# Cached keys turned in 32x32 blocks on VectorE and moved into place by on-chip transfers, instead of 128 TensorE turnings with copies

## The reference

```
ki_past = cache_idx_k[page_table]            # (8, 2048, 64) indexer keys
s     = einsum('bqhd,bsd->bqhs', qi, ki_all) * 64**-0.5
score = einsum('bqh,bqhs->bqs', wi * 8**-0.5, relu(s))
_, sel = top_k(score, 256)
ksel, vsel = cache_k / cache_v rows of sel   # (.., 64)
logits = einsum('bqhd,bqkd->bqhk', q, ksel) * 64**-0.5 ; softmax ; times vsel
```

## Time and profile before

| | |
|---|---|
| median of 3 runs | 1207.28 us |
| the profiled execution | 1206.73 us |
| its span on the core | 1204.9 us |
| mean granted TensorE clock | 0.995 |
| PE busy | 1144.1 us (95%) |
| DVE busy | 374.9 us (31%) |
| ACT busy | 223.7 us (19%) |
| POOL busy | 57.3 us (5%) |
| DMA | 451.92 MB, mean 375 GB/s |

### The profile page before, as it was taken

One profiled execution on the slowest core, in us unless ns is written; L12 is line 12 of the kernel. 1 busy time (PEld: TensorE's weight loads), 2 busy tenths in 40 slices (PEclk: granted clock), 3 DMA queues, 4 the chain that ended last, 5 costly groups with the idle time before them and its releaser, 6 DMA issues.

```text
span 1204.9 us, 15008 instructions
## 1 busy us (share of the span) xinstructions
PE 1144.1 (95%) x5865; PEld 508.8 (42%) x5865; DVE 374.9 (31%) x888; ACT 223.7 (19%) x449; POOL 57.3 (5%) x71
## 2 busy tenths in 40 slices
PE   7998999999999999999999999999989898999997
PEld 6776568773333333333333333333323333333332
DVE  2279942534231322222222223122212222222222
ACT  2236641442111111111111111111111111111102
POOL 2138100000000000000000000000000000000000
PEclk9999999999999999999999999999999999999999
DMA  9345447797999999999999999999999999999994
GB/s 371 106 146 211 168 145 290 297 412 280 404 429 428 426 427 429 426 427 427 428 428 427 427 428 429 426 426 428 428 426 430 427 426 428 427 427 428 429 426 205
DMA packets 44245, 451.92 MB, mean 375 GB/s; under 512 B 5516, under 2 KB 6440, under 8 KB 18055
## 3 DMA queue, kind: packets, MB, share of 16 engines
q1 hardware_dynamic: 41695, 436.94, 86.7%
q0 software_dynamic: 2480, 14.02, 3.1%
HBM read 448.56 MB, written 2.61 MB: 374 GB/s over the span
## 4 chain that ended last, share of the span: by engine, by line
PE 59%; DMA 25%; DVE 12%; ACT 3%; issue 1%; SPq 0%; DVEq 0%; ACTq 0%
DMA mem<-in_w_up_dram 25%; PE psum L1258 20%; PE psum L1295 15%; PE psum L724 4%; PE psum L1245 3%; PE psum L1033 2%; DVE mem L2239 2%; PE psum L1209 2%; PE psum L931 1%; DVE mem L2231 1%; DVE mem L2234 1%; PE psum L1236 1%; ACT mem L1706 1%; DVE mem L2236 1%; PE psum L1223 1%
## 5 line engine op out<-in xcount | busy, mean ns | idle before, releaser
L1258 PE MATMUL psum<-mem 128*64 128x512 f32 x2048 | 457.4, 596 | 13.7 <-DMA mem<-in_w_up_dram 13.2
L1258 PEld LDWEIGHTS psum<-mem 128*64 128x64 f32 x2048 | 142.6, 137 | 303.8 <-issue 274.7
L1295 PE MATMUL psum<-mem 128*64 128x512 f32 x1024 | 236.9, 600 | 0.0
L1295 PEld LDWEIGHTS psum<-mem 128*64 128x64 f32 x1024 | 66.5, 136 | 133.2 <-issue 112.6
L2231 DVE TENSOR_SCALAR mem<-psum 128x512 f32<-128x512 f32 x32 | 22.2, 693 | 275.1 <-PE psum L1258 275.1
L1706 ACT ACTIVATE mem<-mem 128x512 f32<-128x512 f32 x32 | 20.2, 631 | 467.2 <-DVE mem L2231 467.2
L2226 DVE TENSOR_TENSOR mem<-mem,psum 128x528 f32<-128x528 f32 x64 | 45.2, 706 | 130.1 <-PE psum L1245 130.1
L1432 ACT ACTIVATE mem<-psum 128x512 f32<-128x512 f32 (+6 forms) x125 | 61.0, 550 | 97.6 <-PE psum L724 40.9
L1245 PE MATMUL psum<-mem 128*128 128x264 f32 x256 | 65.5, 398 | 0.0
L2216 DVE TENSOR_SCALAR mem<-mem 128x64 f32<-128x64 f32 x99 | 25.0, 312 | 126.9 <-PE psum L1230 99.4
L1201 PE MATMUL psum<-mem 128*64 128x512 f32 x256 | 60.4, 592 | 1.0 <-DVE mem L2147 1.0
(11 more groups left out here) (355 smaller groups left out, 859.8 us busy)
## 6 DMA issues: line engine op xcount, KB each, us to landing
mem<-in_w_up_dram SPq DMA_DIRECT2D x128, 2048.0 KB, 32.5
mem<-in_w_down_dram SPq DMA_DIRECT2D x64, 2048.0 KB, 33.8
mem<-in_w_in_dram SPq DMA_DIRECT2D x8, 868.0 KB, 15.5
mem<-in_cache_mem_k_dram SPq DMA_DIRECT2D x1, 4096.0 KB, 19.9
mem<-in_cache_mem_v_dram SPq DMA_DIRECT2D x1, 4096.0 KB, 15.0
mem<-in_w_o_dram SPq DMA_DIRECT2D x1, 3072.0 KB, 10.9
mem<-in_w_mk_dram SPq DMA_DIRECT2D x2, 1024.0 KB, 6.8
mem<-in_w_mv_dram SPq DMA_DIRECT2D x1, 2048.0 KB, 10.5
```

The source lines that it names most:

```text
L1258: ins = pe.matmul(ps[64 * o:64 * o + 64, :], lhs, w[:, k % 2, g * 1024 + o * 512:g * 1024 + (o + 1) * 512], start=False, stop=(k == 7), sk ...
L1295: ins = pe.matmul(pso[64 * o:64 * o + 64, :], lhs, w[:, k % 4, o * 512:(o + 1) * 512], start=(k == 0), stop=(k == 7), skip_group_check=True)
```

## The change

Nothing is turned on TensorE any more: the jobs `kt`, the buffer `both`, GpSimd's copies and ScalarE's `keep_keys` are gone. `blocks` takes the place of `both`. VectorE's `turn_blocks(q)` makes two transposes per quarter (keys, index keys), each of 128 partitions x 2048 elements, in squares of 32 x 32. A square stays on its 32 partitions, so 16 transfers a quarter, issued by SP, put the squares in place in `KT`: 32 partitions x 4 KB each, from partitions 32g to partitions 32 b4. Columns of `KT` are now (group, position, page), and the views that read them follow. VectorE turns quarter 0 ahead of its first rotation, 1 after the second, 2 after the `QB` copies, 3 between the prompt's two selections. Each waits for the gathers of its quarter and for all transfers of the quarter before (`keys_moved`), since `blocks` has one buffer. SP waits for both transposes, and for quarters 2 and 3 also for `sl` q - 2, which read the same `KT`. GpSimd's gather q waits for the transposes of q - 1. `sample_logits(q)` waits for the transfers of quarter q. In TensorE's order `z` 2 comes ahead of `kin`, `z` 5 ahead of `kvn`, `sl` 0 and 1 ahead of `z` 7 and 8, and `sc` 0 behind the prompt logits.

```diff
@@ -158,15 +158,12 @@
 def psum_jobs():
     js = [("xT", k) for k in range(KD)]
     js += [("z", m) for m in Z_FIRST] + [("rs",)]
-    js += [("z", 1), ("sw", 13), ("sw", 9), ("kin",), ("wr",)] + [("kt", i) for i in range(4)]
-    js += [("z", 2), ("sw", 10), ("sw", 11)] + [("kt", i) for i in range(4, 8)]
-    js += [("z", 3), ("sw", 12), ("sw", 4), ("sw", 0), ("kvn",), ("z", 5), ("sw", 1), ("sw", 2), ("sw", 3)]
-    js += [("kt", i) for i in range(8, 12)] + [("is", 0, g, o) for g in range(2) for o in range(2)]
-    js += [("z", 6)] + [("kt", i) for i in range(12, 16)] + [("is", 1, g, o) for g in range(2) for o in range(2)]
-    js += [("z", 7), ("z", 8)]
-    js += [("sl", 0)] + [("kt", i) for i in range(16, 24)]
-    js += [("sl", 1), ("sc", 0)] + [("kt", i) for i in range(24, 32)]
-    js += [("sl", 2)] + [("lg", 0, g, o) for g in range(2) for o in range(2)]
+    js += [("z", 1), ("sw", 13), ("sw", 9), ("z", 2), ("kin",), ("wr",), ("sw", 10), ("sw", 11), ("z", 3)]
+    js += [("sw", 12), ("sw", 4), ("sw", 0), ("z", 5), ("kvn",), ("sw", 1), ("sw", 2), ("sw", 3)]
+    js += [("is", 0, g, o) for g in range(2) for o in range(2)] + [("z", 6)]
+    js += [("is", 1, g, o) for g in range(2) for o in range(2)]
+    js += [("sl", 0), ("sl", 1), ("z", 7), ("z", 8)]
+    js += [("sl", 2)] + [("lg", 0, g, o) for g in range(2) for o in range(2)] + [("sc", 0)]
     js += [("sc", 1), ("sl", 3), ("sc", 2), ("sln",), ("sc", 3), ("scn",)]
     js += [("vt", i) for i in range(5)] + [("cnt", 0)]
     js += [("st",)] + [("vt", i) for i in range(5, 10)] + [("cnt", 1)]
@@ -322,8 +319,8 @@
         x_nat = unit(14, 3, D)
         x_sq = unit(16, D)
         raw = unit(16, 2, 32, HD)
-        both = unit(14, 32, 2 * HD)
-        KT = [unit(8, P, 32), unit(10, P, 32)]
+        blocks = unit(14, 4, 32, 32)
+        KT = [unit(8, 4, 32, 32), unit(10, 4, 32, 32)]
         prob = [at(home(8), NH, P), at(home(8) + 1024, NH, TP)]
         probT = [at(home(8) + 3072, 1, NH, P), at(home(8) + 4096, 2, NH, P)]
         v_raw = unit(4, P, HD)
@@ -526,6 +523,14 @@
 
             load(new_pool_s[0, :, 0:14, :], state_pool[0, :, 1:15, :], "stored_state")
             w_mk_rows = w_mk[0].rearrange("(k p) h e -> p k (h e)", p=P)
+            for q in range(4):
+                sp.wait_ge(S("keys_turned"), 2 * q + 2)
+                if q >= 2:
+                    wait_filled(sp, "sl", q - 2)
+                for b4 in range(4):
+                    for g in range(4):
+                        sp.dma_start(KT[q % 2][32 * b4:32 * b4 + 32, g], blocks[32 * g:32 * g + 32, b4]
+                                     ).then_inc(S("keys_moved"), 16)
             wait_filled(sp, "sl", 3)
             load(mem_nat, mem_prompt[0].rearrange("(t p) d -> p t d", p=P), "mem_in")
             load(w_mk_lo, w_mk_rows[:, 0:4, :], "w_mk_lo_in")
@@ -627,24 +632,14 @@
             pool.wait_ge(S("squared"), 2)
             pool.wait_ge(S("squared_s"), 1)
             for q in range(4):
+                if q:
+                    pool.wait_ge(S("keys_turned"), 2 * q)
                 gather(raw[:, 0].rearrange("p t d -> p (t d)"), cache_k, q, "raw_k")
                 gather(raw[:, 1].rearrange("p t d -> p (t d)"), cache_idx_k, q, "raw_i")
-                if q == 3:
-                    wait_filled(pool, "z", 8)
-                    for part in range(4):
-                        gather(v_raw[:, 32 * part:32 * part + 32, :].rearrange("p t d -> p (t d)"), cache_v, part,
-                               "raw_v")
-                if q == 0:
-                    for k in range(KD):
-                        wait_filled(pool, "xT", k)
-                else:
-                    wait_filled(pool, "kt", 8 * q - 1)
-
-                pool.wait_ge(S("raw_k"), 16 * q + 16)
-                pool.tensor_copy(both[:, :, 0:HD], raw[:, 0]).then_inc(S("side_by_side"), 1)
-                pool.wait_ge(S("raw_i"), 16 * q + 16)
-                pool.tensor_copy(both[:, :, HD:2 * HD], raw[:, 1]).then_inc(S("side_by_side"), 1)
-                pool.wait_ge(S("side_by_side"), 2 * q + 2)
+            wait_filled(pool, "z", 8)
+            for part in range(4):
+                gather(v_raw[:, 32 * part:32 * part + 32, :].rearrange("p t d -> p (t d)"), cache_v, part, "raw_v")
+
             def linked(ins):
                 pool_steps[0] += 1
                 ins.then_inc(S("pool_step"), 1)
@@ -772,24 +767,13 @@
                             if i == 1:
                                 done(ins, tag, t, g, o)
 
-            def turn_keys(i):
-
-                q = i // 8
-                if i % 8 == 0:
-                    pe.wait_ge(S("side_by_side"), 2 * q + 2)
-                b = take(pe, "kt", i)
-                for j in range(4):
-                    ins = pe.transpose(b[:, j * P:(j + 1) * P], both[:, (4 * i + j) % 32, :], ident)
-                done(ins, "kt", i)
-
             def sample_logits(c):
-                for i in range(8 * c, 8 * c + 8):
-                    wait_drained(pe, "kt", i)
+                pe.wait_ge(S("keys_moved"), 256 * (c + 1))
                 b = take(pe, "sl", c)
                 for s in range(2):
                     for b4 in range(4):
                         n = 4 * s + b4
-                        keys = KT[c % 2][:, n * NPG:(n + 1) * NPG, :].rearrange("p g t -> p (g t)")
+                        keys = KT[c % 2][:, n // 2, :, NPG * (n % 2):NPG * (n % 2) + NPG]
                         ins = pe.matmul(b[32 * b4:32 * b4 + 32, :], QB[:, n, :], keys, start=(s == 0), stop=(s == 1),
                                         skip_group_check=True)
                 done(ins, "sl", c)
@@ -816,6 +800,7 @@
             z_tile(1)
             swap_halves(13)
             swap_halves(9)
+            z_tile(2)
             b = take(pe, "kin")
             wait_drained(pe, "sw", 13)
             wait_drained(pe, "z", 13)
@@ -825,50 +810,37 @@
             done(ins, "kin")
             b = take(pe, "wr")
             done(pe.matmul(b[:, 0:TS], const("head_of_row")[64:72, :], kiT[64:72, TP:NT], start=True, stop=True), "wr")
-            for i in range(4):
-                turn_keys(i)
-            z_tile(2)
             swap_halves(10)
             swap_halves(11)
-            for i in range(4, 8):
-                turn_keys(i)
             z_tile(3)
             swap_halves(12)
             swap_halves(4)
             swap_halves(0)
+            z_tile(5)
             b = take(pe, "kvn")
             wait_drained(pe, "sw", 4)
             wait_drained(pe, "z", 4)
             for t in range(3):
                 ins = pe.transpose(b[0:ROWS[t], t * P:(t + 1) * P], kvT[:, t * P:t * P + ROWS[t]], ident)
             done(ins, "kvn")
-            z_tile(5)
             for m in (1, 2, 3):
                 swap_halves(m)
-            for i in range(8, 12):
-                turn_keys(i)
             for h in range(4):
                 wait_drained(pe, "sw", 9 + h)
             pe.wait_ge(S("key_copies"), 2)
             head_products("is", qiT, kiT, ki2, 0)
             z_tile(6)
-            for i in range(12, 16):
-                turn_keys(i)
             head_products("is", qiT, kiT, ki2, 1)
+            pe.wait_ge(S("qb_ready"), 6)
+            sample_logits(0)
+            sample_logits(1)
             z_tile(7)
             z_tile(8)
-            pe.wait_ge(S("qb_ready"), 6)
-            sample_logits(0)
-            for i in range(16, 24):
-                turn_keys(i)
-            sample_logits(1)
-            sample_score(0)
-            for i in range(24, 32):
-                turn_keys(i)
             sample_logits(2)
             for m in range(4):
                 wait_drained(pe, "sw", m)
             head_products("lg", qT, kvT, k2, 0)
+            sample_score(0)
             sample_score(1)
             sample_logits(3)
             sample_score(2)
@@ -1476,21 +1448,16 @@
                         act.wait_ge(S("zeroed"), 2)
                     copy(UT[:, m - 5, 16:16 + NT], b[:, 0:NT], "z", m)
 
-            def keep_keys(i):
-                b = result(act, "kt", i)
-                i8 = i % 8
-                copy(KT[i // 8 % 2][:, :, 4 * i8:4 * i8 + 4], b[:, :].rearrange("p (t g) -> p g t", t=4), "kt", i)
-
             def keep_logits(c):
                 b = result(act, "sl", c)
                 if c >= 2:
                     wait_filled(act, "sc", c - 2)
                 act.activation(RL[:, c % 2, :], b[:, :], ACT.Relu).then_inc(S("relu_s"), 1)
-                copy(LGq[:, c], b[:, :].rearrange("p (g t) -> p g t", g=NPG), "sl", c)
+                copy(LGq[:, c], b[:, :].rearrange("p (t g) -> p g t", g=NPG), "sl", c)
 
             def keep_scores(c):
                 b = result(act, "sc", c)
-                copy(XSq[:, c], b[:, :].rearrange("p (g t) -> p g t", g=NPG), "sc", c)
+                copy(XSq[:, c], b[:, :].rearrange("p (t g) -> p g t", g=NPG), "sc", c)
 
             def keep_products(t):
                 for n in range(4 * t, 4 * t + 4):
```

(30 more changed lines are left out.)

## The result

The changed kernel takes 1222.35 us, the median of 4 runs (1221.52 to 1225.78), beside 1207.35 of the kernel before in the same comparison: a ratio of 1.0128, 95% interval 1.0113 to 1.0143. It is 15 us slower, and 16.4 us above the 1206.0 forecast. The profiled execution took 1225.78 around a span of 1223.9. That is 3.4 above the median, so the trace is read for its stages and not for its total.

What follows compares the result with a forecast made beforehand. Weight stream bounds the end, so the loop's start counts. VectorE's 41.6 us from 49.4 end pair 3 at 91.0; quarter 3 lands at 101.4, first pass 108.8 instead of 110.0: 1206.0 us, own range 1204 to 1208.5, 8-in-10 range 1201 to 1214.5.

Steps and rivals of the forecast that it cites:

- the frame: Expert loop: nothing changed speeds it; its start, 280.76, moves with the first pass over the sample scores, 110.00 before.
- break-even: Moves of a quarter: no gain or loss at 11.0 us (0.54 a transfer), measurable loss from 12.2.
- VectorE's side: VectorE: turnings 4.45 us a pair, three pairs 13.35 on the path; 4.7 us back without GpSimd's copies.
- the cold clock: Last sample logits on TensorE: at 1.2 GHz after 14 us idle, 1.9 us more, and 0.5 on what follows.
- What comes on SP and the DMA: SP's 16 on-chip transfers a quarter: 10.4 us a quarter, standing on the path three times.
- The issue: SP's queue: 0.38 us for each of 16 transfers and 2.4 to landing, 8.5 us a quarter.
- The rate: Moves of a quarter: 2.1 MB at 254 GB/s, taken as 8.0 us, with 2.4 making 10.4.
- The sharing: GpSimd's gathers share the DMA engines with the moves; nothing was added for it.
- Narrow destination: Rival: transfers writing 32 partitions get half the stream's 420 GB/s, 12.4 us a quarter, 1210.1 us; chance 0.15.
- Late transfers: Rival: at 14 us a quarter, quarters 0 and 3 gate by 3.6 more each, 1214.1 us; chance 0.14.

Runs made afterwards that it cites:

- the run with filler: The changed kernel with 11 matmuls of 512 columns put ahead of the wait of the last sample logits on TensorE: 1220.2 us, ratio 1.0104.
- 128-byte rows: The changed kernel with all 64 transfers, each carrying 128 bytes of its 4 KB rows, the rest of the key buffer zero: 1204.83 us, ratio 0.9974.
- The alternating run: The changed kernel with a quarter's 16 transfers reordered so each next one reads and writes the other half of the partitions: 1215.43 us, ratio 1.0065.

## Why the prediction was wrong

- **Right: the frame.** Nothing here touches the loop; its start moves with the first pass (17.7 and 18.0). What a quarter of moves takes (break-even at 11.0 us by the prediction's sum) was the right question.
- **Right: VectorE's side.** A pair 4.50 (4.45 forecast), pair 0 free, GpSimd's contention mostly gone (L1844 3.61, L1861 0.36, L1853 0.94 beside 0.45 forecast).
- **Right: the cold clock.** 3.64 for the last sample logits (3.8 forecast), shown by the run with filler.
- **Wrong: the step "What comes on SP and the DMA"**, the size of its term. A quarter was put at 10.4 and took 13.6, 20.2, 20.9 and 15.0; that is all of the 18.9 us between 108.8 and 127.72 (see the result). It failed in all three of its factors, and the runs show that they cost together, not one by one:
  - *The issue*, 0.38 from `b_up`, is 0.63 to 0.64 for an on-chip source and 0.46 for HBM in a row of 16. By the prediction's form that is 16 x 0.63 + 2.4 = 12.5 a quarter, over its break-even; measured 11.7 with 128 partitions and no gather. Yet the pace alone cost nothing (1204.83 with 128-byte rows).
  - *The rate*, 254 GB/s, came from half a microsecond in which a store flew beside the two transfers, and those two write partitions 32 to 63 and 64 to 95, one on either side of the middle. In the changed kernel, eight in a row go into partitions 0 to 63 and the next eight into the rest, at 207 GB/s from 43 to 48 us. The alternating run shows the difference: 257 instead of 216 GB/s over the same four microseconds, 7 us of kernel time. The prediction named both flaws of the row, and took its rate all the same.
  - *The sharing*, "for which I add nothing", took the most: 13.25 of the 18.9 us are the waits before pairs 2 and 3, whose quarters are the ones with key gathers beside them. The prediction had those gathers fly at the same time as the moves. VectorE leaves 13.0 us between pairs 1 and 2 and 15.1 between 2 and 3, and the 9.4 us of moves and 7.4 of gathers don't fit in there. Without the key gathers both waits are gone and the kernel is at 1208.1; with half of the bytes they are 1.40 and 0.37 us and it is at 1207.6. So neither the gathers nor the narrow transfers did it alone.
- **The rivals.** "Narrow destination" had the mechanism, 0.62 us for 128 KB, and 51.4 for quarter 0's landing (39.0 + 12.4; measured 50.8). The rule of the Trainium skill that it named ("SBUF — State Buffer", "Door 1: The DMA port swizzle": 32 partitions reach 8 of 16 ports, about 218 GB/s at best) is borne out by 201 to 217 GB/s at a DMA share of 0.97 to 1.03 (windows of 43 to 48 us) and 208 from HBM, against 414 over 128 partitions; the windows right behind the `w_in` stream go from 180 up to 258 (at 0.90), 216 on average from 40 to 44. But the rival gave 1210.1, since it let each quarter fly alone. "Late transfers" had the way the loss adds up: a late quarter 0 and quarter 3 each count in full, and at 20 us quarters 1 and 2 gate too, where it had 0.8 for quarter 1 at 14. It also named the gathers of values beside the moves. The two rivals were one case, and their 0.15 and 0.14 rested on `b_up`, a row that was only nearly the same operation. Both their times (1210.1 and 1214.1) were still too low.
- **The same page** of the Trainium skill, in the section "Can I just issue two DMAs to hit both halves?", says that two transfers to different halves together were measured only 6% faster than one. Here the measurement differs: with 16 in a row, alternating the halves lifts the rate from 216 to 257 GB/s over the same four microseconds, 19%.

What stays open: why the issue of an on-chip transfer is 0.63 and not 0.46 wasn't tried further; whether the read of 32 partitions adds to the write of 32 (transfers from 128 partitions into 32 weren't tried); and why the first window behind the `w_in` stream shows 258 GB/s.
